# V stage of a PEER layer: token tiles as the stationary operand, 512 columns of V as the moving one

## The reference, cut to what matters

```python
h   = rms_norm(x1, norm2_g)
q   = (h @ w_pq).reshape(N, 8, 2, 128)
s   = einsum('nhcd,hckd->nhck', q, sub_keys)
sv, si = top_k(s, 16)                       # per half key
fv, fi = top_k(sums of the two halves, 16)  # 8 heads x 16 = 128 experts per token
g   = softmax(fv)
a   = gelu(einsum('td,ted->te', h, expert_u[eidx]))
y   = x1 + einsum('te,ted->td', g * a, expert_v[eidx])
```

## Time and profile before

| | |
|---|---|
| median of 3 runs | 1066.0 us (1062.39 to 1068.5) |
| profiled execution, its time | 1062.9 us |
| its span | 1061.2 us |
| busy: PE, weight loads (PEld), DVE, ACT, POOL | 98%, 91%, 69%, 41%, 42% |
| granted TensorE clock | 1.00 |
| DMA, mean | 224 GB/s |

### The profile page before, as it was taken

The page is one execution under the profiler, slowest core; times in us unless marked ns, Lnnn a source line. Parts: engine busy times, 40 slices in busy tenths (PEclk is TensorE's granted clock), DMA queues, the critical chain, the costliest instruction groups (busy, mean ns, idle before and its releaser), DMA issues.

```text
span 1061.2 us, 22916 instructions
## 1 busy us (share of the span) xinstructions
PE 1043.6 (98%) x8465; PEld 965.3 (91%) x8465; DVE 732.1 (69%) x1492; ACT 430.9 (41%) x745; POOL 449.0 (42%) x329
## 2 busy tenths in 40 slices
PE   6999999999999999999999999999999999999998
PEld 3447878889999999999999999999999999999998
DVE  2659999469999558888989865755555555555554
ACT  2124231343446544343433345544444444444442
POOL 4753444246688877777778760011111111111100
PEclk9999999999999999999999999999999999999999
DMA  9444569268655578888888866676666666666663
GB/s 336 110 134 144 167 203 344 74 243 305 228 186 180 178 234 296 278 278 281 276 281 271 293 222 195 218 274 227 219 210 216 217 229 226 220 218 213 211 214 105
DMA packets 79963, 237.60 MB, mean 224 GB/s; under 512 B 11750, under 2 KB 24686, under 8 KB 79493
## 3 DMA queue, kind: packets, MB, share of 16 engines
q1 hardware_dynamic: 65564, 195.51, 55.6%
q0 software_dynamic: 13040, 40.52, 11.4%
q10 hardware_dynamic: 1280, 0.53, 0.2%
HBM read 233.56 MB, written 3.14 MB: 223 GB/s over the span
## 4 chain that ended last, share of the span: by engine, by line
PE 88%; DVE 9%; DMA 1%; issue 1%; POOL 1%; ACT 0%; DVEq 0%
PE psum L1041 34%; PE psum L973 34%; PE psum L984 5%; PE psum L567 4%; DVE top L1557 3%; DVE work_s L1558 2%; PE psum L803 2%; PE psum L1055 2%; PE psum L776 1%; PE psum L551 1%; PE psum L925 1%; PE psum L583 1%; PE psum L746 1%; DVE work_p L1558 1%; PE psum L557 1%
## 5 line engine op out<-in xcount | busy, mean ns | idle before, releaser
L1461 POOL TENSOR_TENSOR w_lo<-w_raw,w_hi 128x1024 fp32r<-128x1024 f32 x116 | 282.7, 2442 | 104.2 <-ACT w_hi L1074 103.2
L1074 ACT ACTIVATE w_hi<-w_raw 128x1024 fp32r<-128x1024 f32 x214 | 226.9, 1060 | 228.2 <-PE psum L1041 105.2
L973 PE MATMUL psum<-h_hi,w_hi 128*128 128x256 f32 x1024 | 296.5, 290 | 0.3 <-issue 0.3
L1041 PE MATMUL psum<-ag_hi,w_hi 128*128 128x256 f32 x1024 | 291.6, 285 | 0.5 <-DVE ag_lo L1805 0.5
L1041 PE MATMUL psum<-ag_lo,w_hi 128*128 128x256 f32 x1024 | 289.7, 283 | 0.0
L973 PE MATMUL psum<-h_hi,w_lo 128*128 128x256 f32 x1024 | 289.5, 283 | 0.0
L973 PE MATMUL psum<-h_lo,w_hi 128*128 128x256 f32 x1024 | 289.5, 283 | 0.0
L1041 PEld LDWEIGHTS psum<-ag_hi,w_hi 128*128 128x128 f32 x1024 | 196.3, 192 | 7.3 <-issue 6.6
L973 PEld LDWEIGHTS psum<-h_hi,w_hi 128*128 128x128 f32 x1024 | 196.0, 191 | 2.1 <-issue 1.7
L1041 PEld LDWEIGHTS psum<-ag_lo,w_hi 128*128 128x128 f32 x1024 | 196.4, 192 | 0.0
L973 PEld LDWEIGHTS psum<-h_lo,w_hi 128*128 128x128 f32 x1024 | 196.3, 192 | 0.0
(11 more groups left out here) (283 smaller groups left out, 1418.8 us busy)
## 6 DMA issues: line engine op xcount, KB each, us to landing
w_raw<-expert_ut SPq DMA_DIRECT2D x128, 512.0 KB, 4.5
w_raw<-expert_v SPq DMA_DIRECT2D x86, 512.0 KB, 3.8
raw_more<-expert_v SPq DMA_DIRECT2D x42, 512.0 KB, 4.2
w_slice<-w_pq_cols SPq DMA_DIRECT2D x32, 512.0 KB, 5.6
rows_in<-h_save SPq DMA_DIRECT2D x32, 512.0 KB
w_most<-w_in_blocks SPq DMA_DIRECT2D x8, 699.0 KB, 12.2
w_slice<-w_o_half SPq DMA_DIRECT2D x8, 512.0 KB, 4.4
v_cache<-cache_v POOLq DMA_DIRECT2D x64, 64.0 KB, 3.4
```

The costliest lines, as they stand in the source:

```text
L973: mm = pe.matmul(psum[:, 2 + s, 0:SEQ], a[:, s, c, :], b[:, c, :], start=(i == 0), stop=(i == 3 * KC - 1))
L1041: mm = pe.matmul(y_bank(c), a[:, c, :], b, start=(first and i == 0 and c not in (1, 3)), stop=(last and i == 2), skip_group_check=True)
L1074: return act.activation(out, in_, ACT.Copy)
L1461: pool.tensor_tensor(w_lo[:, s], w_raw[:, s], w_hi[:, s].bitcast(F32), ALU.subtract).then_inc(S["w_lo_ready"], 1)
```

## The change

In the V stage the operands change places. For each step and each of two tiles of 128 tokens (t), the activations stand still and half of V's channels, 512 columns (h), move: 2 x 2 x 3 = 12 matmuls. The result y now has tokens on the partitions, in four whole banks (6, 7, 0, 1), so step 0 no longer waits for banks 4 and 5. The wait for the low part of V stands behind the first eight matmuls of a step. The residual isn't added by DVE at the end but by PE: in step 20, 16 fp32 matmuls with a 128 x 128 piece of x_res as the stationary operand and the identity as the moving one add x1, turned, into the same banks. At the end two banks are copied by DVE and two by ACT to y_out (in the place of `store`'s first rows), and SP stores them in four pieces of 256 KB to y_p, token-major. The sample tokens go on as before; their result goes to y_s.

```diff
+    y_out = at("y_out", F0, [P, 2, D])
+    X1_AT = NU + 20
+    Y_ORDER = ((0, 0), (0, 1), (1, 0), (1, 1))
-    def y_bank(c):
-        return psum[:, (6, 6, 7, 7, 0, 1, 4, 5)[c], (c % 2 if c < 4 else 0) * SEQ:(c % 2 + 1 if c < 4 else 1) * SEQ]
+    def y_bank(i):
+        return psum[:, (6, 7, 0, 1)[i], :]
...
             sp.wait_ge(S["y_added"], 1)
-            sp.dma_start(y_t[:, :, SEQ:NT], x_res[:, :, SEQ:NT]).then_inc(S["out_done"], 16)
-            for c in range(0, KC, 2):
-                sp.wait_ge(S["y_added"], c + 3)
-                sp.dma_start(y_t[:, c:c + 2, 0:SEQ], x_res[:, c:c + 2, 0:SEQ]).then_inc(S["out_done"], 16)
-            sp.wait_ge(S["out_done"], 16 * (2 + KC // 2))
+            sp.dma_start(y_s, x_res[:, :, SEQ:NT]).then_inc(S["out_done"], 16)
+            for i, (t, h) in enumerate(Y_ORDER):
+                if h == 0:
+                    sp.wait_ge(S["y_added"], 2 + t)
+                else:
+                    sp.wait_ge(S["y_copied"], 1 + t)
+                sp.dma_start(y_p[t, :, BANK * h:BANK * (h + 1)], y_out[:, t, BANK * h:BANK * (h + 1)]
+                             ).then_inc(S["out_done"], 16)
+            sp.wait_ge(S["out_done"], 16 * (2 + len(Y_ORDER)))
...
             def prod_v(v, first=False, last=False):
                 s = v % RING
-                hi, lo, a_hi, a_lo = w_hi[:, s], v_low(v), ag_hi[:, s, :], ag_lo[:, v % 2, :]
                 pe.wait_ge(S["w_hi_ready"], NU + v + 1)
-                low_in(NU + v)
                 pe.wait_ge(S["ag_hi_ready"], v + 1)
                 pe.wait_ge(S["ag_lo_ready"], v + 1)
                 if first:
                     pe.wait_ge(S["g_done"], G_STEPS)
-                for c in range(KC):
-                    if first and c >= 6:
-                        pe.wait_ge(S["act_free"], NU + (c - 7))
-                    i = 0
-                    for a, b in ((hi, a_hi), (hi, a_lo), (lo, a_hi)):
-                        mm = pe.matmul(y_bank(c), a[:, c, :], b, start=(first and i == 0 and c not in (1, 3)),
-                                       stop=(last and i == 2), skip_group_check=True)
-                        i += 1
+                def term(i, a, b, start=False, stop=False):
+                    t, h = Y_ORDER[i]
+                    return pe.matmul(y_bank(i), a[:, t * P:(t + 1) * P],
+                                     b[:, 4 * h:4 * h + 4, :].rearrange("p c d -> p (c d)"), start=start, stop=stop,
+                                     skip_group_check=True)
+                for t in range(2):
+                    for h in range(2):
+                        term(2 * t + h, ag_hi[:, s, :], w_hi[:, s], start=first)
+                    for h in range(2):
+                        term(2 * t + h, ag_lo[:, v % 2, :], w_hi[:, s])
+                low_in(NU + v)
+                for i in range(len(Y_ORDER)):
+                    mm = term(i, ag_hi[:, s, :], v_low(v), stop=last)
                     if last:
                         mm.then_inc(S["y_psum"], 1)
                 if not last:
                     mm.then_inc(S["prod_done"], 1)
+            def residual():
+                pe.wait_ge(S["x_res_in"], 16)
+                for i, (t, h) in enumerate(Y_ORDER):
+                    for c in range(4):
+                        pe.matmul(y_bank(i)[:, c * P:(c + 1) * P], x_res[:, 4 * h + c, t * P:(t + 1) * P], ident[:, :],
+                                  start=False, stop=False, skip_group_check=True)
...
+                if NU + v == X1_AT:
+                    residual()
...
+            for i, (t, h) in enumerate(Y_ORDER):          (ACT, at its end)
+                if h == 1:
+                    act.wait_ge(S["y_psum"], i + 1)
+                    copy(y_out[:, t, BANK * h:BANK * (h + 1)], y_bank(i)).then_inc(S["y_copied"], 1)
...
-            for c in range(KC):                            (DVE, at its end)
-                dve.wait_ge(S["y_psum"], (2, 2, 4, 4, 5, 6, 7, 8)[c])
-                dve.tensor_tensor(x_res[:, c, 0:SEQ], x_res[:, c, 0:SEQ], y_bank(c), ALU.add
-                                  ).then_inc(S["y_added"], 1)
+            for i, (t, h) in enumerate(Y_ORDER):
+                if h == 0:
+                    dve.wait_ge(S["y_psum"], i + 1)
+                    dve.tensor_copy(y_out[:, t, BANK * h:BANK * (h + 1)], y_bank(i)).then_inc(S["y_added"], 1)
```

More of the change, by code:

```diff
@@ L84, in hybrid_kernel @@
                   c_fold, c_own, c_ident, c_iota,
-                  y_t, k_prompt, v_prompt, ik_prompt, pool_prompt,
+                  y_p, y_s, k_prompt, v_prompt, ik_prompt, pool_prompt,
                   k_sample, v_sample, ik_sample, pool_sample):
@@ L1893 @@
     a.update(shape_constants(SEQ, DB, DS, PAST, (D - PW) // HD, HD, IH, ID, NST))
-    outs = [("y_t", (P, D // P, SEQ + DB * DS)),
+    outs = [("y_p", (2, P, D)), ("y_s", (P, D // P, DB * DS)),
             ("k_prompt", (1, 1, SEQ, HD)), ("v_prompt", (1, 1, SEQ, HD)), ("ik_prompt", (1, 1, SEQ, ID)),
@@ L1902 @@
     r = run_bass_kernel_spmd(nc, [a], core_ids=[0])
-    y = np.ascontiguousarray(r.results[0]["y_t"].transpose(2, 1, 0)).reshape(SEQ + DB * DS, D)
-    return (y[:SEQ].reshape(1, SEQ, D), y[SEQ:].reshape(DB, DS, D)) + tuple(r.results[0][n] for n, _ in outs[1:])
+    y = np.ascontiguousarray(r.results[0]["y_p"]).reshape(1, SEQ, D)
+    y_s = np.ascontiguousarray(r.results[0]["y_s"].transpose(2, 1, 0)).reshape(DB, DS, D)
+    return (y, y_s) + tuple(r.results[0][n] for n, _ in outs[2:])
```

## The result

The changed kernel takes 1052.7 us (median of 4 runs, 1049.6 to 1056.6) against 1064.2 us of the kernel before (4 runs): ratio 0.989, 95% interval 0.984 to 0.994. So it is 11 us faster; the forecast was 31.7.

The account below looks back on a forecast made before the run. The prediction took TensorE's V-stage product stream as the bound: products -37.2, first steps +0.6, residual +3.8, end +1.1, sum -31.7 us from the 1066.0 us median, giving 1034 us; range 1029 to 1068.

Parts of the forecast that it names:

- What bounds the kernel: TensorE in the V stage: a stream of 3,072 matmul instructions priced by their start-to-start pitch, 120 ns; 34% of the span.
- The products, -37.2 us: V stage: 12 products of 512 columns a step at 215.8 ns replace 24 at 120.0 ns, saving 290 ns x 128.
- Rival A: V products: 13.3 ns excess is per instruction, or load slows columns beside it; pitch 226.7 ns, 1050.7 us; chance 0.22.
- Rival B: V products: excess belongs to the 4-byte columns; pitch 237.5 ns, 3.8 us gained, 4.9 paid, 1067.1 us; chance 0.12.
- C: V products: pitch just twice 120 ns, nothing gained, added work paid; 1070.9 us, 0.46% slower; chance 0.13.
- The first steps, +0.6 us: Start of V: steps 0 and 1 end 2 x 0.29 us earlier, but the wait before step 2 grows by as much.
- The residual, +3.8 us: Step 20 of V: 32 fp32 instructions at 113 ns, 3.6 us, plus some 0.2 us for two changes of type.
- The end, +1.1 us: After the last product: all four banks finish late, so stores taking 2.9 us end 1.0 to 1.1 us later than before.
- The DMA, 0 us: V stage: transfers of V blocks and sample rows keep up with the shorter steps; 0 us, up to 3 us for the range.

## Why the prediction was wrong, point by point

**What bounds the kernel**: right. TensorE's stream in V, step after step, but for the stops told above; in the kernel before the stage repeats to 0.2 us.

**The products, -37.2 us: this step failed.** It said "after, if the load hides as in L776: 213.3 + 2.5 = 215.8 ns", and chose the fp32 row as the nearest. That row hides its load, but it draws a column every two cycles. The pitch is 226.7 ns: 10.9 ns x 1,536 products = 16.7 us less, so 20.5 us. The reading behind it, that the 13.3 ns of an fp32r product are the pace of its load, was half right: 6.3 ns go with a shorter load, 6.8 are the columns' own, and they grow with the columns: about twice as much, 13.4, at 512, where a shorter load saves nothing (with narrow weights even 16.7, so the split isn't exact). The wide product does away with the load's share: 24 x 6.3 = 151 ns of the 160 that a step gained. Rival A named the right pitch and a time 2 us off. Of its two causes the price per instruction fails, since it would not fall at 256 with narrow weights; the load that slows the columns beside it has the 6.3 ns at 256 for it and the 512 columns, where a narrower load saves nothing, against it. Rival B had the right place for half of it. Two sums of the prediction are off by little: 30 ns a step are 3.8 us, not 3.9, and B with half of C has a chance of 0.185, not 0.17.

**A term that was missing, +1.4 us.** After each of the 16 groups of sample rows the seven steps take together 19.31 - 7 x 2.72 = 0.27 us more than steady ones, before 20.34 - 7 x 2.88 = 0.18. These 0.09 us each were not in the sum; what makes them stays open. They belong to the width, since with 256 columns and exchanged operands the seven steps take 20.34 us.

**The first steps, +0.6 us**: right in kind. Step 2 began 6.6 us after the last U product before, and 7.2 and 6.4 us after it in the two traces of the changed kernel; by its chain it waits for a load that scatters. With the 0.3 us by which steps 0 and 1 are shorter that gives back 0.9 us in the first trace and 0.1 in the second. The stop stood in two parts in the first trace (675.78 and 681.93 above).

**The residual, +3.8 us**: 3.6 in the chain, 3.4 by leaving it out. Right. The 0.2 us for two changes of type didn't show: 32 instructions take 3.57 us and the step behind them 2.73 us instead of 2.72.

**The end, +1.1 us**: 1.2 in both traces. The mechanism is right, four stores that start late and then flow at the DMA's rate, as the run that starts them earlier shows. That the size came out is in part luck: the transfer flows 0.9 us after the first issue, not "0.4 us after the issue, as now" (before, too: issue at 1056.47 us, and the prediction's own 2.9 us of transfer ending at 1060.3 began at 1057.4), and against it the stores moved at 410 GB/s instead of 365, 2.6 us instead of 2.9.

**The DMA, 0 us**: nearly. The transfers kept up, except for a V block that landed late after 8.3 to 8.9 us in both traces of the changed kernel, while x_res and sample rows were being loaded. The seven steps around it took 20.44 and 19.86 us instead of 19.31: 1.1 and 0.6 us. That moving the load of x_res cures this is likely and not shown.

With the measured terms the first trace has -20.5 + 1.4 + 0.9 + 3.6 + 1.2 + 1.1 = -12.3 us, the second -20.5 + 1.4 + 0.1 + 3.6 + 1.2 + 0.6 = -13.6 us, where the traces have -11.9 and -13.6. Of the rest in the first, 0.2 us is one block of seven steps, at 742 us, that took 19.53 us instead of 19.31; why isn't known.

## What to carry to other kernels

A surcharge per instruction read at one width has at least two parents, the load of the weights and the columns themselves, and only a row of the same number format at another width tells them apart; a row of another format that draws its columns at half the rate doesn't. Where the gain rests on such a number, take the middle of the bounds as the forecast or measure the pitch of the one form first, which costs a block of 48 products. When the last step of an accumulation finishes all banks together, the stores that used to hide behind it come after it; ordering that one step bank by bank brings them back.

## What the hardware showed that was not expected

- fp32r products at the 2.4 GHz level take 6 to 10% more than one cycle per column from 320 columns on (146.9 ns for 320, 226.7 for 512 with 128-wide weights), and 12% at 256. Of the same shapes, bf16 products stay within 2.6 ns of one cycle per column, fp32 instructions within 2.6 ns of two.
- With 512 fp32r columns moving, narrower weights are slower: 226.7 ns at 128 wide, 230.6 at 96, 229.8 at 64, 231.9 at 32.
- The granted clock fell to the 1.2 GHz level while TensorE was issuing without a gap: at about 1085 us, after 48 products of 64 moving columns and at the start of products that use only 64 rows; it stayed there through the products of 64 and 32 rows and was back at 1.00 in the stretch from 1166 us, under products of 128 rows. In the V stage it stood at 1.00 throughout.
- The part ahead of the V stage scatters by 12 us between executions of identical work (last U product at 667.8 to 679.5 us), while the V stage repeats to 0.2 us in the kernel before.
